# Merge of two branches formed in four spare PSUM banks, its rounded part made by ScalarE, and the next product started on every fourth merged block

## The chip, the cores and the metric

The kernel runs on one core of a Trainium2 chip. The metric is the device time of one execution, in microseconds (us). An engine here is TensorE (PE; its weight loads have a row of their own, PEld), VectorE (DVE), ScalarE (ACT), GpSimd (POOL) or SyncE (SP).

## What is computed

The reference runs two transformer-like blocks on 256 tokens of width 2048, all in fp32. The change is in the second block, at the place where two branches meet and go through an output product:

```python
merged = jax.nn.sigmoid(gate_ret) * (ret @ w_br_ret[l]) + jax.nn.sigmoid(gate_dil) * (dil @ w_br_dil[l])
x = x + merged @ w_out[l]
```

`ret` is 256 x 1024, `dil` is 256 x 512, `w_out` is 2048 x 2048. Ahead of it lie the first block, the projections, the retention and the dilated attention; behind it lie a cross attention to a memory of 256 tokens and a large expert layer, which is more than half of the time.

## The kernel before, in words

**Layout.** Activations are kept transposed: 128 partitions of the width by 256 tokens, `KC` = 16 such blocks for a width of 2048. A weight matrix is streamed as tiles of 1 MB (128 x 2048 numbers). SP loads them in one long order (`STREAM`) into a ring of four slots, and reloads a slot once both halves of its tile have been split.

**Split weights.** Products are made of a rounded part and a remainder. For each half of a tile (8 pieces of 128 x 128) ACT copies the half into `w_hi`, rounded (`split_half`, L1174; the copy is L1180), POOL forms `w_lo` = tile - `w_hi` (L427), and PE then runs the half. `w_hi` and `w_lo` have four places, so ACT may split a half once PE has done the half four before it (the wait on `half_done` in `split_half`). Activations are split in the same way into `h_hi` and `h_lo`. `half_wide` (L489) multiplies the rounded weight by both parts of the activation in one matmul of 512 columns (L495) and the remainder weight by the rounded part in one of 256 (L497). `half` (L478) does the same with three matmuls of 256 columns (L484, L485, L486).

**The stages around the change.** They follow each other in the weight stream: `gate`, `br_ret` (8 tiles), `br_dil` (4 tiles), `out2` (16 tiles), `kv`. PE holds results in PSUM banks 0 to 3, and DVE frees them by counting `bank_free`.
- In `gate`, 32 blocks are made into `pg`, and ACT puts a sigmoid on them.
- In `br_ret`, each half of a tile gives one block. DVE adds the two halves of its bank into a buffer `mrg` (L1718) and multiplies it by the gate in place in `pg` (L2449).
- In `br_dil` (PE from L1002), each half of a tile gives two blocks, of four pieces each. Half m (0 to 7) gives blocks 2m and 2m+1, in banks 2m mod 4 and 2m+1 mod 4. Before it writes block k, PE waits until DVE has read block k-4 out of the same bank.
- DVE (L2452 to L2468) takes each block k through four instructions, one after another, each behind a wait for the one ahead of it: the product of the bank and the gate into `mrg` (L2457), which frees the bank; the sum with the other branch, in `mrg` (L2459); the rounded copy into `h_hi` (L2461); the remainder into `h_lo` (L2463). The names `h_hi` and `h_lo` are parts of `hc_hl`, and so the trace calls them. Behind block 15 it raises `merged`.
- PE waits for `merged` (L1011), and then runs the 16 tiles of `out2` (`tile`, L530), each of which needs all 16 blocks of `h_hi` and `h_lo`. After each tile, DVE adds both halves of the bank to `x` (`added`, L2470; L2473 and L2475).
- ACT splits the weights of `br_dil` (L1517) and then those of `out2`, two tiles ahead of PE. Behind the third tile of `out2` it waits for `merged` and starts on the norm of the memory (L1520 on), whose arrays overlay `pg`.

Banks 4 to 7 of PSUM are not used from the end of the dilated attention until the norm of the memory, which uses bank 7 after the thirteenth tile of `out2`.

Of the kernel before, what the change touches and what calls it, by code (L numbers as in the profile page):

```python
# [19 lines left out]
F32 = mybir.dt.float32  # L20
# [4 lines left out]
ALU = mybir.AluOpType  # L25
ACT = mybir.ActivationFunctionType
# [3 lines left out]
T = 256  # L30
D = 2048
KC = D // P
# [52 lines left out]
FIRST = {}  # L85
# [3 lines left out]
RING = 4  # L89
# [30 lines left out]
def build(nc, a, out):  # L120
    ctx = ExitStack()

    def sem(name):
        return ctx.enter_context(nc.semaphore(name))

    psum = ctx.enter_context(nc.psum_tensor("psum", [P, 8, 512], F32))
# [23 lines left out]
    h_hl, c_hl = hc_hl[:, 0], hc_hl[:, 1]  # L150
    h_hi, h_lo, c_hi, c_lo = h_hl[:, 0], h_hl[:, 1], c_hl[:, 0], c_hl[:, 1]
# [93 lines left out]
    pg = at("pg", [P, GATE_TILES, T], 120)  # L245
    mrg = at("mrg", [P, 2, T], 200)
# [48 lines left out]
    bank_free, acc_free = sem("bank_free"), sem("acc_free")  # L295
# [36 lines left out]
    d_sc, d_mx, d_e, d_p, d_tp, d_pt, d_o, d_hi, d_lo = (sem("dil_" + n) for n in (  # L332
        "scores", "max", "exp", "prob", "turned", "prob_turned", "out", "hi", "lo"))
    s_sig = sem("gates_sigmoid")
    merged = sem("merged")
    k_half = sem("keys_done")
    m_tp, m_vn, m_sc, m_mx, m_e, m_p, m_pt_, m_pc, m_o, m_hi, m_lo = (sem("mem_" + n) for n in (
        "v_turned", "v_natural", "scores", "max", "exp", "prob", "turned", "prob_turned", "out", "hi", "lo"))
# [138 lines left out]
    def _(pe):  # L477
# [49 lines left out]
                                      start=s == 0, stop=s == 1)  # L527
            m.then_inc(norm_sum, 1)

        def tile(name, n, hl, after=None):  # L530

            pe.wait_ge(bank_free, bank_of[name] + n + 1)

            def moving(k):
                if after is not None and n == 0 and k % 4 == 0:
                    pe.wait_ge(norm_lo, 4 * NS[after] + k // 4 + 1)
                return hl[:, :, k]
            for h in range(2):
                half_wide(FIRST[name] + n, n % RING, h, lambda c: h == 0 and c == 0,
                          lambda c: h == 1 and c == KC // 2 - 1, lambda c: n % RING, lambda c: moving(h * 8 + c))  # L540
# [5 lines left out]
        for i in range(ADA_G):  # L546
            pe.wait_ge(ada_copied, i + 1)
            for j in range(RING):
                pe.wait_ge(landed[j], 16 * i + 16)
                wide = ring[:, j].rearrange("p k n -> p (k n)")  # L550
                for k in range(4):
                    m = pe.matmul(psum[0:2, 4 + i % 2, :], c_silu[:, 4 * j + k], wide[:, 512 * k:512 * k + 512],  # L552
                                  start=j + k == 0, stop=j + k == 6)
# [8 lines left out]
        for n in range(ADA_1):  # L562
            m = pe.transpose(psum[:, 6, 2 * n:2 * n + 2], mod_rows[:, n * P:n * P + P], const[0:2, IDENT, 0:2])
# [19 lines left out]
        for t in range(XBC):  # L583
            pe.wait_ge(bank_free, bank_of["xbc"] + t + 1)
            for h in range(2):
# [3 lines left out]
                for c in range(8):  # L589
                    k = h * 8 + c  # L590
# [4 lines left out]
                    m = pe.matmul(o, w_lo[:, slot, c], hc_hl[:, :, 0, k], start=False, stop=k == KC - 1)  # L595
# [47 lines left out]
        for g in range(2):  # L643
            for tb in range(2):
                m = pe.transpose(psum[:, 0, (2 * g + tb) * P:(2 * g + tb + 1) * P],
                                 xbc[:, 8 + g, 1, tb * P:tb * P + P], sq(IDENT))
# [8 lines left out]
        for c0, d, parts in sums:  # L655
            for n, (mat, tb) in enumerate(parts):
                m = pe.matmul(psum[:, 4, c0:c0 + 16], sq(mat), da[:, tb, d], start=n == 0, stop=n == len(parts) - 1)
# [4 lines left out]
        for n in range(4):  # L662
# [3 lines left out]
            for tb in range(2):  # L666
                pe.wait_ge(ssd_xw, 2 * n + tb + 1)
                m = pe.matmul(psum[:, (2, 6)[n % 2], :], b_nat[:, g, tb], xw[:, tb, :], start=tb == 0, stop=tb == 1)
# [67 lines left out]
        for g in range(2):  # L736
            for k in range(4):
                m = pe.matmul(psum[:, 6, g * T:g * T + T], sq(ONES), y_sq[:, 4 * g + k], start=k == 0, stop=k == 3)
# [232 lines left out]
        for m_ in range(2 * DIL_HG):  # L971
            h, tb = m_ // 2, m_ % 2
# [3 lines left out]
            for g in range(DIL_G):  # L976
                for s in range(tb + 1):
                    n = g * (tb + 1) + s
                    m = pe.transpose(flat[:, n * P:n * P + P], dil_s[:, m_ % 2, T * g + P * s:T * g + P * s + P],
                                     sq(IDENT))  # L980
# [5 lines left out]
            for n in range(last + 1):  # L986
                g, s = n // (tb + 1), n % (tb + 1)
                m = pe.matmul(psum[:, 2 + h % 2, tb * P:tb * P + P], v_dil[:, s, 4 * g + h], dil_pt[:, n],
                              start=n == 0, stop=n == last)
# [13 lines left out]
        for j in range(RING):  # L1003
            for h in range(2):
                def target(c):
                    if c % 4 == 0:
# [1 line left out]
                    return psum[:, 2 * h + c // 4, 0:T]  # L1008
                half(g0 + j, j, h, lambda c: c % 4 == 0, lambda c: c % 4 == 3, target,
                     lambda c: dil_hi[:, c % 4], lambda c: dil_lo[:, c % 4])  # L1010
        pe.wait_ge(merged, 1)  # L1011
        for n in range(KC):
            tile("out2", n, h_hl)
            if n == 12:
                norm_pe("mem", column=True)
        for n in range(KC):
# [6 lines left out]
        for n in range(8):  # L1023
# [3 lines left out]
            for k in range(4):  # L1027
                m = pe.transpose(psum[:, n % 2, k * P:k * P + P], kv[:, KC + 4 * g + k, mb * P:mb * P + P], sq(IDENT))
# [13 lines left out]
        for h in range(MEM_H):  # L1042
# [5 lines left out]
            for mb in range(2):  # L1048
                for tb in range(2):
                    m = pe.transpose(psum[:, h % 2, mb * T + tb * P:mb * T + tb * P + P],  # L1050
                                     mem_e[:, h % 2, tb, mb * P:mb * P + P], sq(IDENT))
# [4 lines left out]
            for c in range(4):  # L1056
                for mb in range(2):
                    m = pe.matmul(psum[:, 2 + c // 2, (c % 2) * T:(c % 2) * T + T], v_mem[:, mb, 4 * h + c],
                                  mem_pt[:, h % 2, mb], start=mb == 0, stop=mb == 1)
# [111 lines left out]
    def _(act):  # L1171
        st = Steps(act, act_step)
# [14 lines left out]
        def split_stage(name, first=0, n=None, ahead=0):  # L1187

            g0, n = FIRST[name] + first, n or dict(STREAM)[name]
            for s in range(ahead, RING if ahead else 0):  # L1190
                split_tile(g0 + s, g0 // RING, s)
            with act.Fori(1 if ahead else 0, n // RING) as i:
                for s in range(RING):
                    split_tile(i * RING + (g0 + s), i + g0 // RING, s)
# [59 lines left out]
        for q in range(4):  # L1254
            for k in range(4 * q, 4 * q + 4):
                m = act.activation(c_hi[:, k], ctx_raw[:, k], ACT.Identity, scale=scales[:, 1, k:k + 1],
                                   bias=mod[:, k, 1:2])
# [167 lines left out]
        def split_at(g):  # L1425
            split_tile(g, g // RING, g % RING)
# [28 lines left out]
        for n in range(2, RET_TILES + 2):  # L1455
# [11 lines left out]
            if n >= 14 and n % 2 == 0 and n <= 28:  # L1467
                h = (n - 14) // 2
# [14 lines left out]
        for m_ in range(2 * DIL_HG):  # L1483
            h, tb = m_ // 2, m_ % 2
            keys = P * (tb + 1)
            act.wait_ge(d_mx, m_ + 1)
            s, n = (t_[:, m_ % 2] for t_ in (dil_s, dil_n))
# [26 lines left out]
        split_tile(FIRST["br_ret"] + 2, FIRST["br_ret"] // RING, 2)  # L1514
        split_tile(FIRST["br_ret"] + 3, FIRST["br_ret"] // RING, 3)
        split_stage("br_ret", RING, KC // 2 - RING)
        split_stage("br_dil")  # L1517
        act.wait_ge(norm_in, 64)

        def gained_squared(name, src, hi, k):  # L1520
# [9 lines left out]
                m.then_inc(norm_sq, 1)  # L1530

        for n in range(KC):
            split_at(FIRST["out2"] + n)
            if n == 2:
                act.wait_ge(merged, 1)
            if 2 <= n < 10:
                gained_squared("mem", mem_raw, mem_hi, 2 * n - 4)
                gained_squared("mem", mem_raw, mem_hi, 2 * n - 3)
# [14 lines left out]
        for h in range(MEM_H):  # L1553
            act.wait_ge(m_mx, h + 1)
            for tb in range(2):
                m = act.activation(mem_e[:, h % 2, tb], psum[:, 4 + h % 2, tb * T:tb * T + T], ACT.Exp,
                                   bias=mem_n[:, h % 2, tb:tb + 1], scale=r_col[:, CROSS, tb:tb + 1],
                                   accum_out=mem_n[:, h % 2, 2 + tb:3 + tb])
# [109 lines left out]
    def _(dve):  # L1668
# [782 lines left out]
        st.settle()  # L2451
        g0 = FIRST["br_dil"]  # L2452
        dve.wait_ge(bank_free, 4 + bank_of["br_dil"])
        for k in range(KC):
            dve.wait_ge(half_done, 2 * g0 + k // 2 + 1)
            t_, m_ = mrg[:, 0], mrg[:, 1]
            dve.tensor_tensor(t_, psum[:, k % 4, 0:T], pg[:, KC + k], ALU.mult).then_inc(bank_free, 1)  # L2457
            dve.wait_ge(bank_free, 4 + bank_of["br_dil"] + k + 1)
            st.did(dve.tensor_tensor(m_, t_, pg[:, k], ALU.add))  # L2459
            st.settle()  # L2460
            st.did(dve.tensor_copy(h_hi[:, k], m_))  # L2461
            st.settle()
            m = dve.tensor_tensor(h_lo[:, k], m_, h_hi[:, k].bitcast(F32), ALU.subtract)  # L2463
            if k < KC - 1:
                st.did(m)
                st.settle()
        m.then_inc(merged, 1)
        dve.wait_ge(merged, 1)  # L2468

        def added(name, n):  # L2470

# [413 lines left out]
```

## Time and profile before

| | us |
|---|---|
| median of 3 runs | 4730.65 (4725.55 to 4736.2) |
| the profiled execution, its own time | 4737.4 |
| span of the profiled execution, first to last instruction | 4735.6 |
| `br_dil` and the merge: PE's first matmul of it to its first of `out2` | 2457.12 to 2503.77 |

Every position in the tables further down is in microseconds from the start of the span. A row of the timeline gives start, duration, engine, line, operation, the output and the inputs by name, and in brackets how long the engine had stood idle before it and which instruction released it. "PEclk" is the TensorE clock that was granted in a stretch, as a share of full speed.

### The profile page before, as it was taken

What the parts mean: (1) busy time and instruction counts of PE and PEld (TensorE: products, weight loads), DVE (VectorE), ACT (ScalarE), POOL (GpSimd) and SP (SyncE); (2) the same over time, 40 slices, a digit from 0 to 9 for tenths busy, and PEclk for the clock granted to TensorE, in tenths of its full rate; (3) what the DMA queues carried; (4) which work ended last, traced back from release to release, by engine and by line L of the source; (5) the groups of instructions that cost most, each with busy time, mean ns of one, the idle gap of its engine ahead of it and who ended that gap; (6) DMA issues with size and microseconds to landing.
All of it is one profiled execution on the core that took longest, in us unless ns stands there. A gap on an engine that the chain in (4) does not pass through costs nothing.

```text
span 4735.6 us, 65884 instructions
## 1 busy us (share of the span) xinstructions
PE 4394.2 (93%) x24574; PEld 3679.7 (78%) x24574; DVE 2613.2 (55%) x3813; ACT 1731.0 (37%) x1875; POOL 3294.6 (70%) x1312
## 2 busy tenths in 40 slices
PE   8898988789999989996998998999999899999997
PEld 1676755678888878884887786889888788888876
DVE  3325775355545664314244512398867856875784
ACT  1234422333333343431543432443333333333433
POOL 0347740678888877881876783797887787788776
PEclk9998979889999999997999999999999999999999
DMA  8346750445445544551544452444454454454443
GB/s 312 123 183 243 300 189 9 151 161 183 180 179 184 181 157 160 184 186 45 187 177 142 166 189 98 169 170 161 177 185 171 159 186 172 161 180 177 173 163 125
DMA packets 111109, 804.92 MB, mean 170 GB/s; under 512 B 12903, under 2 KB 13192, under 8 KB 14088
## 3 DMA queue, kind: packets, MB, share of 16 engines
q1 hardware_dynamic: 108720, 787.30, 45.8%
q10 hardware_dynamic: 2200, 14.90, 0.9%
q8 instruction: 142, 2.33, 0.2%
q14 instruction: 47, 0.39, 0.0%
HBM read 800.06 MB, written 2.10 MB: 169 GB/s over the span
## 4 chain that ended last, share of the span: by engine, by line
PE 41%; POOL 29%; issue 21%; DVE 8%; ACT 1%; DMA 1%; POOLq 0%; DVEq 0%; SPq 0%; ACTq 0%
POOL w_lo L427 28%; PE psum L495 18%; PE psum L497 9%; PE psum L610 3%; PE psum L552 2%; DVE out_hl L2679 2%; DVE out_hl L2677 1%; DVE hid L2675 1%; POOL ada_acc L455 1%; PE psum L1104 1%; PE psum L593 1%; PE psum L484 1%; PE psum L595 1%; PE psum L594 1%; PE psum L485 1%
## 5 line engine op out<-in xcount | busy, mean ns | idle before, releaser
L427 POOL TENSOR_TENSOR w_lo<-ring,w_hi 128x1024 fp32r<-128x1024 f32 x1216 | 2944.3, 2425 | 1286.4 <-ACT w_hi L1180 1285.5
L1180 ACT ACTIVATE w_hi<-ring 128x1024 fp32r<-128x1024 f32 x1240 | 1310.2, 1060 | 2146.8 <-PE psum L497 1887.6
L495 PE MATMUL psum<-hc_hl,w_hi 128*128 128x512 f32 x5184 | 1852.6, 401 | 86.4 <-DVE hc_hl L2138 24.5
L497 PE MATMUL psum<-hc_hl,w_lo 128*128 128x256 f32 x5184 | 1453.8, 280 | 0.0
L495 PEld LDWEIGHTS psum<-hc_hl,w_hi 128*128 128x128 f32 x5184 | 982.0, 189 | 325.3 <-issue 55.9
L497 PEld LDWEIGHTS psum<-hc_hl,w_lo 128*128 128x128 f32 x5184 | 985.8, 190 | 2.0 <-issue 1.9
L495 PE MATMUL psum<-out_hl,w_hi 128*128 128x512 f32 x2048 | 725.0, 398 | 30.3 <-DVE x L2689 27.4
L497 PE MATMUL psum<-out_hl,w_lo 128*128 128x256 f32 x2048 | 577.5, 282 | 0.0
L495 PEld LDWEIGHTS psum<-out_hl,w_hi 128*128 128x128 f32 x2048 | 387.6, 189 | 123.1 <-DVE x L2689 28.3
L497 PEld LDWEIGHTS psum<-out_hl,w_lo 128*128 128x128 f32 x2048 | 390.7, 191 | 0.0
L495 PE MATMUL psum<-hid_hl,w_hi 128*128 128x512 f32 x1024 | 367.0, 402 | 19.6 <-DVE hid_hl L2192 12.2
L455 POOL TENSOR_TENSOR ada_acc<-ada_acc,ada_row 128x2048 f32<-128x2048 f32 x56 | 256.1, 4574 | 70.3 <-ACT ada_row L1291 64.8
L497 PE MATMUL psum<-hid_hl,w_lo 128*128 128x256 f32 x1024 | 289.0, 282 | 0.0
L495 PEld LDWEIGHTS psum<-hid_hl,w_hi 128*128 128x128 f32 x1024 | 194.6, 190 | 70.8 <-DVE hid_hl L2192 14.5
L2687 DVE TENSOR_TENSOR x<-psum,x 128x256 f32<-128x256 f32 x256 | 108.0, 422 | 245.7 <-PE psum L497 245.1
L610 PE MATMUL psum<-x,ring 128*128 128x256 f32 x1024 | 233.9, 389 | 8.7 <-DMA ring<-mixed 5.7
L610 PEld LDWEIGHTS psum<-x,ring 128*128 128x128 f32 x1024 | 197.5, 195 | 46.0 <-DMA ring<-mixed 8.2
L2677 DVE CAST out_hl<-hid 128x256 fp32r<-128x256 f32 x128 | 221.9, 1733 | 4.4
L2199 DVE SCALAR_TENSOR_TENSOR x<-psum,mod,x 128x256 f32<-128x256 f32 x224 | 108.4, 484 | 201.7 <-PE psum L497 197.7
L497 PEld LDWEIGHTS psum<-hid_hl,w_lo 128*128 128x128 f32 x1024 | 195.5, 191 | 0.0
L495 PE MATMUL psum<-mem_hl,w_hi 128*128 128x512 f32 x512 | 181.0, 399 | 9.4 <-POOL w_lo L427 9.4
L1291 ACT ACTIVATE ada_row<-ring,c_silu 128x2048 f32<-128x2048 f32 x64 | 126.7, 1998 | 80.2 <-DMA ring<-mixed 53.7
(440 smaller groups left out, 5559.1 us busy)
## 6 DMA issues: line engine op xcount, KB each, us to landing
ring<-stream SPq DMA_DIRECT2D x652, 1024.0 KB, 4.8
ring<-mixed SPq DMA_DIRECT2D x96, 1024.0 KB, 6.3
x<-x ACTq DMA_DIRECT2D x2, 2048.0 KB, 11.2
ctx_raw<-ctx ACTq DMA_DIRECT2D x1, 2048.0 KB, 9.8
mem_raw<-mem ACTq DMA_DIRECT2D x1, 2048.0 KB, 7.8
out<-x SPq DMA_DIRECT2D x4, 512.0 KB, 2.6
filt_w<-filt_w ACTq DMA_DIRECT2D x1, 1024.0 KB, 11.0
dft<-dft ACTq DMA_DIRECT2D x1, 1024.0 KB, 12.9
```

What stands on the lines that cost most here:

```text
L427: pool.tensor_tensor(w_lo[:, slot], ring[:, s, k], w_hi[:, slot].bitcast(F32), ALU.subtract).then_inc(lo_ready, 1)
L455: pool.tensor_tensor(ada_acc[:, n % 2], ada_row[:, 0] if k == 1 else ada_acc[:, n % 2], ada_row[:, k % 2], ALU.add).then_inc(ada_done, 2 i ...
L495: pe.matmul(psum[:, b, :].rearrange("p (s t) -> p s t", s=2), w_hi[:, slot, c], x_hl, start=start(c), stop=False, skip_group_check=True)
L497: m = pe.matmul(psum[:, b, 0:T], w_lo[:, slot, c], x_hl[:, 0], start=False, stop=stop(c), skip_group_check=True)
L552: m = pe.matmul(psum[0:2, 4 + i % 2, :], c_silu[:, 4 * j + k], wide[:, 512 * k:512 * k + 512], start=j + k == 0, stop=j + k == 6)
L610: m = pe.matmul(psum[:, (3, 7)[i % 2], 0:T], ring[:, (3 * i) % RING, k], x[:, k], start=k == 0, stop=k == KC - 1)
L1180: act.activation(w_hi[:, 2 * (s % 2) + h], ring[:, s, k], ACT.Copy).then_inc(hi_ready, 1)
L1291: act.activation(ada_row[:, t % 2], w, ACT.Copy, scale=c_silu[:, t % KC, 0:1]).then_inc(ada_scaled, 1)
L2199: dve.scalar_tensor_tensor(x[:, d], psum[:, 4 + d % 4, s * T:s * T + T], mod[:, gate + d, 0:1], x[:, d], ALU.mult, ALU.add).then_inc(acc_f ...
L2677: st.did(dve.tensor_copy(out_hi[:, j], hid[:]))
L2679: dve.tensor_tensor(out_lo[:, j], hid[:], out_hi[:, j].bitcast(F32), ALU.subtract).then_inc(hid_ready, 1)
L2687: st.did(dve.tensor_tensor(x[:, d], psum[:, 4 + d % 4, 0:T], x[:, d], ALU.add))
```

## The change

The merged block is no longer formed in `mrg`. DVE writes the product of bank and gate into one of PSUM's banks 4 to 7 (block k in bank 4 + k mod 4) and adds the other branch there in place. ACT makes the rounded part `h_hi` out of that bank, and DVE makes `h_lo` from the bank and `h_hi`, three blocks later than the sum. A bank is written again once the `h_lo` of four blocks before is done. `merged` now counts blocks, and PE, in the first tile of `out2`, waits for 4, 8, 12 and 16 of them, at every fourth piece. ACT's splits of `br_dil` and of the first two tiles of `out2` are written out as 12 halves, and behind the halves 5 to 11 the rounded copies of two blocks each are put (blocks 2m-10 and 2m-9 behind half m), the last two blocks behind those.

```diff
-    merged = sem("merged")
+    merged, br_sum, br_hi = sem("merged"), sem("branches_summed"), sem("branches_hi")
...
-        def tile(name, n, hl, after=None):
+        def tile(name, n, hl, after=None, each=None):
 
             pe.wait_ge(bank_free, bank_of[name] + n + 1)
 
             def moving(k):
                 if after is not None and n == 0 and k % 4 == 0:
                     pe.wait_ge(norm_lo, 4 * NS[after] + k // 4 + 1)
+                if each is not None and n == 0 and k % 4 == 0:
+                    pe.wait_ge(each, k + 4)
                 return hl[:, :, k]
...
-        pe.wait_ge(merged, 1)
         for n in range(KC):
-            tile("out2", n, h_hl)
+            tile("out2", n, h_hl, each=merged)
...
-        split_stage("br_dil")
+
+        def merged_high(q):
+
+            for k in (2 * q, 2 * q + 1):
+                act.wait_ge(br_sum, k + 1)
+                act.activation(h_hi[:, k], psum[:, 4 + k % 4, 0:T], ACT.Copy).then_inc(br_hi, 1)
+
+        for n in range(RING + 2):
+            for h in range(2):
+                split_half(FIRST["br_dil"] + n, n % RING, h, h == 0)
+                if n >= 2 and 2 * n + h > 4:
+                    merged_high(2 * n + h - 5)
+        merged_high(7)
...
         for n in range(KC):
-            split_at(FIRST["out2"] + n)
+            if n >= 2:
+                split_at(FIRST["out2"] + n)
             if n == 2:
-                act.wait_ge(merged, 1)
+                act.wait_ge(merged, KC)
...
+        def merged_low(k):
+
+            dve.wait_ge(br_hi, k + 1)
+            dve.tensor_tensor(h_lo[:, k], psum[:, 4 + k % 4, 0:T], h_hi[:, k].bitcast(F32), ALU.subtract).then_inc(merged, 1)
+
         for k in range(KC):
             dve.wait_ge(half_done, 2 * g0 + k // 2 + 1)
-            t_, m_ = mrg[:, 0], mrg[:, 1]
-            dve.tensor_tensor(t_, psum[:, k % 4, 0:T], pg[:, KC + k], ALU.mult).then_inc(bank_free, 1)
+            if k >= 4:
+                dve.wait_ge(merged, k - 3)
+            both_branches = psum[:, 4 + k % 4, 0:T]
+            dve.tensor_tensor(both_branches, psum[:, k % 4, 0:T], pg[:, KC + k], ALU.mult).then_inc(bank_free, 1)
             dve.wait_ge(bank_free, 4 + bank_of["br_dil"] + k + 1)
-            st.did(dve.tensor_tensor(m_, t_, pg[:, k], ALU.add))
-            st.settle()
-            st.did(dve.tensor_copy(h_hi[:, k], m_))
-            st.settle()
-            m = dve.tensor_tensor(h_lo[:, k], m_, h_hi[:, k].bitcast(F32), ALU.subtract)
-            if k < KC - 1:
-                st.did(m)
-                st.settle()
-        m.then_inc(merged, 1)
-        dve.wait_ge(merged, 1)
+            dve.tensor_tensor(both_branches, both_branches, pg[:, k], ALU.add).then_inc(br_sum, 1)
+            if k >= 3:
+                merged_low(k - 3)
+        for k in range(KC - 3, KC):
+            merged_low(k)
+        dve.wait_ge(merged, KC)
```

## Rows read from the trace of the kernel before

**Rows 1.** The page, busy time of each engine over the whole span.

```profile
PE 4394.2 (93%) x24574; PEld 3679.7 (78%) x24574; DVE 2613.2 (55%) x3813; ACT 1731.0 (37%) x1875; POOL 3294.6 (70%) x1312
```

**Rows 2.** Windows by stage: length, busy time of each engine, PEclk, DMA share, GB/s.

```profile
2430.00:2457.00 27.00, 27.00 (x157) 23.61 (x156) 10.85 (x20) 10.20 (x10) 23.82 (x11) 1.00 0.54 190
2457.00:2503.90 46.90, 30.15 (x195) 28.43 (x193) 42.38 (x66) 9.52 (x9) 22.95 (x10) 0.82 0.36 130
...
2470.50:2476.30 5.80, 4.80 (x22) 4.80 (x23) 5.35 (x14) 1.06 (x1) 0.70 (x1) 0.50 0.05 23
...
2503.70:2507.00 3.30, 3.23 (x10) 2.74 (x11) 0.02 (x1) 0.00 (x0) 0.00 (x0) 0.50 0.18 77
```

**Rows 3.** Waits from 2457 to 2512: us in total, times, longest us.

```profile
PE psum L484 <- DVE mrg L2457: 9.3, 6, 2.1
...
PE psum L495 <- DVE hc_hl L2463: 7.3, 1, 7.3
```

**Rows 4.** The tile `mrg`: count, duration ns min/median/max, first and last start.

```profile
L2457 DVE TENSOR_TENSOR mrg<-psum,pg x16: 424/424/425, 2460.3 to 2502.0; 128x256 f32<-128x256 f32 x16
L2459 DVE TENSOR_TENSOR mrg<-mrg,pg x16: 424/425/2266, 2460.7 to 2502.5; 128x256 f32<-128x256 f32 x16
L2461 DVE CAST hc_hl<-mrg x16: 293/294/2368, 2461.3 to 2503.0; 128x256 fp32r<-128x256 f32 x16
L2463 DVE TENSOR_TENSOR hc_hl<-mrg,hc_hl x16: 424/426/2596, 2461.6 to 2503.3; 128x256 fp32r<-128x256 f32 x16
```

**Rows 5.** Timeline of DVE in `br_dil`.

```profile
2460.29 0.42 DVE L2457 TENSOR_TENSOR mrg<-psum,pg 128x256 f32<-128x256 f32 x1 [1.61 <-PE psum L486]
...
2461.59 2.51 DVE L2463 TENSOR_TENSOR hc_hl<-mrg,hc_hl 128x256 fp32r<-128x256 f32 x1
...
2464.60 2.27 DVE L2459 TENSOR_TENSOR mrg<-mrg,pg 128x256 f32<-128x256 f32 x1
...
2483.86 0.42 DVE L2457 TENSOR_TENSOR mrg<-psum,pg 128x256 f32<-128x256 f32 x1
...
2485.56 0.42 DVE L2457 TENSOR_TENSOR mrg<-psum,pg 128x256 f32<-128x256 f32 x1
...
2503.29 0.43 DVE L2463 TENSOR_TENSOR hc_hl<-mrg,hc_hl 128x256 fp32r<-128x256 f32 x1
```

**Rows 6.** Timeline of POOL in `br_dil`.

```profile
2461.39 2.44 POOL L427 TENSOR_TENSOR w_lo<-ring,w_hi 128x1024 fp32r<-128x1024 f32 x1 [0.44 <-ACT w_hi L1180]
2464.20 2.38 POOL L427 TENSOR_TENSOR w_lo<-ring,w_hi 128x1024 fp32r<-128x1024 f32 x1 [0.38 <-ACT w_hi L1180]
```

**Rows 7.** Timeline of PE: first matmuls of halves 0 and 1, of `out2` tiles 0 and 1.

```profile
2457.12 0.28 PE L484 MATMUL psum<-dil_hi,w_hi 128*128 128x256 f32 x1
...
2459.99 0.28 PE L484 MATMUL psum<-dil_hi,w_hi 128*128 128x256 f32 x1
...
2503.77 0.79 PE L495 MATMUL psum<-hc_hl,w_hi 128*128 128x512 f32 x1 [7.25 <-DVE hc_hl L2463]
...
2510.96 0.40 PE L495 MATMUL psum<-hc_hl,w_hi 128*128 128x512 f32 x1
```

**Rows 8.** Timeline of DVE behind two later tiles of `out2`.

```profile
2522.25 0.42 DVE L2473 TENSOR_TENSOR x<-psum,x 128x256 f32<-128x256 f32 x1 [4.67 <-PE psum L497]
...
2527.80 0.42 DVE L2473 TENSOR_TENSOR x<-psum,x 128x256 f32<-128x256 f32 x1 [4.66 <-PE psum L497]
2528.26 0.42 DVE L2475 TENSOR_TENSOR x<-psum,x 128x256 f32<-128x256 f32 x1
2528.60 3.04 DVE L2207 SCALAR_TENSOR_TENSOR mem_hl<-mem_raw,cols,mem_hl 128x256 fp32r<-128x256 f32 x2
```

**Rows 9.** Groups by shape: xcount, busy us, mean ns, idle before.

```profile
L1180 ACT ACTIVATE w_hi<-ring 128x1024 fp32r<-128x1024 f32 x1240 | 1310.2, 1060 | 2146.8 <-PE psum L497 1887.6 <-PE psum L486 151.4 <-PE psum L595 81.2
...
L1492 ACT ACTIVATE dil_hi<-psum 128x256 fp32r<-128x256 f32 x4 | 1.5, 383 | 41.5 <-PE psum L988 41.5
...
L2633 DVE TENSOR_TENSOR psum<-psum,gate_t 128x256 f32<-128x256 f32 x2 | 0.9, 432 | 0.1
```

## The prediction

> **What bounds the kernel now.** I began with the page: PE is busy for 93% of the span and POOL for 70% [rows 1]. An average over a long kernel says little of one stage, so I cut the stretch around the merge into windows [rows 2]. From 2430 to 2457 PE is busy for 27.00 of 27.00 us at a granted clock of 1.00: `br_ret` runs at PE's pace. From 2457 to 2503.9 PE is busy for only 30.15 of 46.90 us at a clock of 0.82, while DVE is busy for 42.38. So DVE sets the pace of `br_dil`. The waits say where [rows 3]: six times PE's first matmul of a half or of its second block waits for DVE's L2457, which frees a bank (9.3 us), and `out2` then waits 7.3 us for the last remainder, L2463.
>
> Why is DVE slow? Where nothing disturbs it, one block takes 1.70 us (2483.86 to 2485.56) [rows 5], so two blocks take 3.40 us, and PE makes two in 2.87 us (2457.12 to 2459.99) [rows 7]. DVE is the slower one even then. Sixteen blocks would take 27.2 us. They took 2460.29 to 2503.72 = 43.4 us [rows 5]. The other 16.2 us are in eight instructions that last some 2 us longer than their like: four times L2463, twice L2459, twice L2461. Rows 4 show it by the distance of maximum and median (2596 against 426 ns, 2266 against 425, 2368 against 294). Two of the eight stand in rows 5 (2461.59 and 2464.60), and they end at 2464.10 and 2466.87, just behind POOL's subtractions, which end at 2463.83 and 2466.58 [rows 6]. All eight go with a POOL subtraction in this way. L2457 is never among them: 424, 424, 425 ns for all 16 [rows 4]. It is the one of the four that reads PSUM and so has one input in SBUF. The others read only SBUF.
>
> PE pays twice more. After its waits the clock granted is 0.50, that is 1.2 in place of 2.4 GHz, from 2470.5 to 2476.3 and again in the first tile of `out2` [rows 2], which takes 7.19 us (2503.77 to 2510.96) [rows 7] where a tile takes 5.55 us (2522.25 to 2527.80) [rows 8].
>
> **The change, part by part.**
>
> *DVE.* Four instructions per block become three, and each of the three reads one input from PSUM. Product and sum write to PSUM from PSUM and SBUF. L2633 has exactly this form and size and takes 432 ns [rows 9]; L2457, the nearest form of the remainder's, takes 424 ns [rows 4]. An instruction that waits for the one ahead starts 0.46 us after it (2527.80 to 2528.26), one that doesn't 0.34 us (2528.26 to 2528.60) [rows 8]. The sum waits for the product, the remainder three blocks back waits for nothing fresh, and the next product waits for that remainder: 0.46 + 0.34 + 0.46 = 1.26 us a block, 2.52 us a half. If all three steps are full ones it is 1.38 and 2.76 us. Both lie below PE's 2.87 us, so DVE no longer holds a bank back. I take the eight long instructions as gone, because L2457 meets POOL in the same stretch and never shows one. If they stay, see the third case.
>
> Rows put reads from PSUM and from SBUF at the same 424 ns [rows 4]. The Trainium skill (VectorE: DVE Perf Modes, section on the TRN2 errata) states a fixed part of 120 cycles for a PSUM source and 58 for an SBUF source, which is 65 ns apart and speaks against moving two instructions of each block to PSUM. By that page, as an estimate, DVE would need up to 3.02 us a half, and the sum below would be some 1.5 us smaller. The measured 424 ns decides here.
>
> *ACT.* It takes on 16 rounded copies out of PSUM. The nearest row, `dil_hi` from PSUM, is 383 ns [rows 9]. With its split of 1.06 us [rows 9] ACT has 1.06 + 2 x 0.38 = 1.83 us to do in each 2.87 us, and in this stretch it was busy for only 9.52 of 46.90 us [rows 2]. The copies of half q stand behind the split of half q+5, which waits until PE has done half q+1. DVE asks for the first of them at block 2q+3, which is of half q+1 too, behind five other instructions, some 2.1 us after that half's end, and ACT needs 1.06 + 0.38 = 1.4 us. So DVE waits for nothing, or for tenths of a us. What is queued behind a copy is the next split, and behind that POOL and PE. POOL's remainder for half 4 is done at 2463.83 [rows 6] where PE, unhindered, needs it at 2457.12 + 4 x 2.87 = 2468.6. That is 4.8 us of reserve against at most 0.8 us of copies. Cost on the path: nothing; without that cover it would be 16 x 0.38 = 6.1 us.
>
> *PE.* Eight halves of 2.87 us end at 2480.08. The first tile of `out2` can start at once. It asks for remainders 0 to 7 (long done), 8 to 11 at 2480.08 + 2.77 = 2482.85 and 12 to 15 at 2480.08 + 4.16 = 2484.24. DVE starts on the last half's blocks 0.30 us behind PE, as it did at 2460.29 behind 2459.99, so at 2480.38. Remainder 11 is its third instruction there, done at 2481.6; remainder 15 is the ninth, done between 2484.0 and 2484.5. PE waits 0 to 0.3 us. The second tile then starts at 2480.08 + 5.55 = 2485.63, plus up to 0.3.
>
> *POOL, SP and the DMAs.* No subtraction or load is added. SP reloads a slot on POOL's remainder, and POOL must hold 2.87 us a half with 2.4 us of work [rows 6], as it did through `br_ret`. DMA was busy for a share of 0.54 at that full pace [rows 2], so loads do not bind when they come closer together.
>
> *Behind it.* The norm of the memory waits for tiles of `out2`, and everything after moves with them. I cost it at nothing.
>
> **The sum.** The second tile of `out2` starts at 2510.96 before [rows 7] and at 2485.6 to 2485.9 after, so 25.0 to 25.3 us are saved. It can be split into the 16.6 us of waits [rows 3], the 1.6 us that the first tile takes too long, and 7.1 us left for matmuls of `br_dil` at the clock of 0.50 and for gaps that no wait names. I take 25. Against the profiled execution's own 4737.4 us it gives 4712. That execution lies 6.8 us above the median of the three runs, 4730.65, and from the median it gives 4705.7, say 4706, which is my number.
>
> **The rivals.**
>
> *DVE stays the bound, mildly.* If a write to PSUM and its read back by the next instruction cost more than rows 8 show, say 0.55 us a step (0.09 above the full one; L2633, at 8 ns above L2457, speaks for the lower end), 48 steps take 26.4 us. The last remainder is done at 2486.7 and the second tile starts 1.4 us later, at 2488.1. The saving is 22.9 us: 4708, or some 4710 if PE's short waits bring the clock of 0.50 back for a few us.
>
> *The long instructions stay.* If POOL's subtractions hold one DVE instruction each, eight times 2.03 us come on top of 16 x 1.26 = 20.2 us: the last remainder at 2497.0, four pieces at half the clock (2 x 1.39 us), tile 1 at about 2499.8. The saving is 11.2 us: 4719. The 16 undisturbed L2457 speak against it.
>
> *The hand-over closes into a ring, and it is slower.* Place: ACT's queue, where copies wait for DVE's sums, DVE's next product for the remainder, the remainder for the copy, and the copy for a split that waits for PE. Should the three and five halves of distance not hold, one turn is PE 2.87 + DVE 2.76 + ACT 1.83 = 7.5 us a half. Eight of them and a tile are 65.5 us against 53.8 now (2457.12 to 2510.96), so 11.7 us slower: 4742. It decides from 6.0 us a half on. Against it: each wait reaches back at least three blocks.
>
> *The change does what it says and something behind takes it back.* DVE and POOL meet at other moments in the following stages, each meeting being worth 2 us (two instructions take 3.04 us at 2528.60 [rows 8]). A few more or fewer on a path that PE waits for are plus or minus 5 us, and I put this into the range. That nothing changes at all would need PE not to start `out2` early and DVE not to be faster. I see no way but a share of this case.
>
> **How the numbers follow.** Forecast 0.79, DVE mildly bound 0.09, long instructions stay 0.05, ring 0.02, taken back behind 0.05 (4715 to 4730). A measurement of this kernel tells about 0.2%, 9.5 us, from no change, so faster means under 4721. The first two cases lie there wholly, the third mostly: faster 0.93, the same 0.05, slower 0.02. The range: the three runs spread over 10.7 us, so a median may be off by some 4; with the 5 us behind, 4698 at the low end. At the high end 4719 takes in the dearer DVE and reaches the third case.
>
> **What would show it.** Right: three DVE instructions a block with none above 0.5 us in `br_dil`; block to block 1.26 to 1.38 us, with DVE waiting for PE at each half; copies near 0.38 us on ACT; PE from 2457 on busy throughout at a clock of 1.00, about 28.5 us from the first matmul of `br_dil` to the second tile of `out2`; no wait of PE on the merge above 0.5 us. Wrong: DVE instructions of 2 us again (third case), DVE rows waiting for ACT's copy by more than 1 us each half (ring), product and sum rows well above 432 ns (second), or a stretch behind `out2` that has grown.

## The result, and the profile after

The changed kernel takes 4708.25 us (median of 6 runs, 4702.76 to 4710.33) against 4733.42 us for the kernel before (6 runs, 4725.55 to 4737.32): 25.2 us less, a ratio of 0.9946 with a 95% interval of 0.9934 to 0.9958.

Below, "the passage" is the time from PE's first matmul of `br_dil` to its first of the second `out2` tile. It was 53.84 us before [rows 7]. Windows of the changed kernel (length, busy time of PE, PEld, DVE, ACT, POOL, then PEclk, DMA share, GB/s), the first of which is the passage:

```profile
2459.30:2488.20 28.90, 28.90 (x227) 28.16 (x226) 19.95 (x50) 15.09 (x26) 24.40 (x11) 1.00 0.52 183
2430.00:2457.00 27.00, 27.00 (x158) 23.80 (x157) 10.59 (x20) 9.89 (x11) 23.90 (x10) 1.00 0.54 194
2488.20:2511.00 22.80, 22.80 (x131) 19.76 (x131) 8.35 (x12) 14.31 (x25) 19.43 (x9) 1.00 0.53 188
2511.00:2533.00 22.00, 12.91 (x69) 10.96 (x68) 8.47 (x12) 7.75 (x14) 7.37 (x4) 0.84 0.22 86
```

PE was busy for 30.15 of 46.90 us at a clock of 0.82 [rows 2]. It is now busy for all 28.90 us at 1.00. DVE fell from 42.38 us of work to 19.95, ACT rose to 15.09, and neither sets the pace. The timeline of PE gives the corners of the passage (start, duration, engine, line, operation):

```profile
2459.33 0.28 PE L484 MATMUL psum<-dil_hi,w_hi 128*128 128x256 f32 x1
...
2482.36 0.40 PE L495 MATMUL psum<-hc_hl,w_hi 128*128 128x512 f32 x1
...
2488.01 0.40 PE L495 MATMUL psum<-hc_hl,w_hi 128*128 128x512 f32 x1
```

The eight halves take 23.03 us and the first tile of `out2` 5.65, so the passage is 28.68 us, 25.2 shorter. No wait of PE stands between them. Two blocks on DVE, from its timeline, to be laid beside [rows 5]:

```profile
2468.16 0.43 DVE L2478 TENSOR_TENSOR psum<-psum,pg 128x256 f32<-128x256 f32 x1 [0.86 <-PE psum L486]
2468.63 0.43 DVE L2480 TENSOR_TENSOR psum<-psum,pg 128x256 f32<-128x256 f32 x1
2468.97 0.41 DVE L2471 TENSOR_TENSOR hc_hl<-psum,hc_hl 128x256 fp32r<-128x256 f32 x1
2469.49 0.43 DVE L2478 TENSOR_TENSOR psum<-psum,pg 128x256 f32<-128x256 f32 x1
2469.95 0.43 DVE L2480 TENSOR_TENSOR psum<-psum,pg 128x256 f32<-128x256 f32 x1
2470.30 0.41 DVE L2471 TENSOR_TENSOR hc_hl<-psum,hc_hl 128x256 fp32r<-128x256 f32 x1
2471.04 0.43 DVE L2478 TENSOR_TENSOR psum<-psum,pg 128x256 f32<-128x256 f32 x1 [0.33 <-PE psum L486]
```

The brackets (the idle time in front of an instruction, and what ended it) have changed sides. Before, PE waited for DVE; now DVE waits for PE at each half, 1.61, 1.08 and 0.86 us at the first three (the first blocks have no remainder of an earlier block beside them), and 0.33 us from the fourth on. A block costs 1.33 us (2468.16 to 2469.49), and no instruction is long. The groups of the passage by shape (xcount, busy us, mean ns, idle before):

```profile
L2480 DVE TENSOR_TENSOR psum<-psum,pg 128x256 f32<-128x256 f32 x16 | 6.9, 432 | 0.6
L2478 DVE TENSOR_TENSOR psum<-psum,pg 128x256 f32<-128x256 f32 x16 | 6.9, 431 | 5.8 <-PE psum L486 5.2
...
L2471 DVE TENSOR_TENSOR hc_hl<-psum,hc_hl 128x256 fp32r<-128x256 f32 x16 | 6.4, 414 | 0.0
...
L1523 ACT ACTIVATE hc_hl<-psum 128x256 fp32r<-128x256 f32 x16 | 5.1, 373 | 0.4 <-DVE psum L2480 0.4
```

The profiled execution has a span of 4706.6 us, 29.0 less than before. Of that, 25.2 us lie in the passage. The passage starts 2.2 us later than before, and 6.0 us come from behind it. Those 6.0 us look like scatter and no part of the gain: in a second profile of the same kernel (span 4719.5 us) the stretch behind the passage is 8.1 us longer than before. The last section says where such differences come from.

### The profile page after: what moved, and what is told of

It is laid out like the page before. It is cut to its first block, busy times and chain, and to the rows that moved or that the text cites. A ratio compares the mean times of both kernels' runs of the same rounds, so it can differ in the third digit from the quotient of the medians.

```text
span 4706.6 us, 65879 instructions
## 1 busy us (share of the span) xinstructions
PE 4380.9 (93%) x24574; PEld 3673.3 (78%) x24574; DVE 2596.1 (55%) x3797; ACT 1735.5 (37%) x1891; POOL 3297.6 (70%) x1312
## 4 chain that ended last, share of the span: by engine, by line
PE 41%; POOL 29%; issue 21%; DVE 8%; DMA 1%; ACT 1%; POOLq 0%; DVEq 0%; SPq 0%; ACTq 0%
POOL w_lo L427 28%; PE psum L495 18%; PE psum L497 9%; PE psum L612 3%; PE psum L554 2%; DVE out_hl L2696 2%; DVE out_hl L2694 1%; DVE hid L2692 1%; PE psum L1105 1%; PE psum L595 1%; PE psum L596 1%; PE psum L597 1%; PE psum L484 1%; PE psum L485 1%; PE psum L486 1%
## 5 line engine op out<-in xcount | busy, mean ns | idle before, releaser
L495 PE MATMUL psum<-hc_hl,w_hi 128*128 128x512 f32 x5184 | 1853.7, 401 | 79.3 <-DVE hc_hl L2152 24.5
L495 PEld LDWEIGHTS psum<-hc_hl,w_hi 128*128 128x128 f32 x5184 | 980.8, 189 | 317.6 <-issue 55.7
L495 PE MATMUL psum<-out_hl,w_hi 128*128 128x512 f32 x2048 | 719.9, 395 | 31.8 <-DVE x L2706 28.4
L495 PEld LDWEIGHTS psum<-out_hl,w_hi 128*128 128x128 f32 x2048 | 387.3, 189 | 119.5 <-DVE x L2706 29.4
L495 PE MATMUL psum<-hid_hl,w_hi 128*128 128x512 f32 x1024 | 368.2, 403 | 18.9 <-DVE hid_hl L2206 12.2
L495 PEld LDWEIGHTS psum<-hid_hl,w_hi 128*128 128x128 f32 x1024 | 195.0, 190 | 70.6 <-DVE hid_hl L2206 14.4
L495 PE MATMUL psum<-mem_hl,w_hi 128*128 128x512 f32 x512 | 181.0, 399 | 9.4 <-POOL w_lo L427 9.4
## 6 DMA issues: line engine op xcount, KB each, us to landing
filt_w<-filt_w ACTq DMA_DIRECT2D x1, 1024.0 KB, 10.9
dft<-dft ACTq DMA_DIRECT2D x1, 1024.0 KB, 12.9
```

The lines of the kernel that those rows point to most:

```text
L495: pe.matmul(psum[:, b, :].rearrange("p (s t) -> p s t", s=2), w_hi[:, slot, c], x_hl, start=start(c), stop=False, skip_group_check=True)
```

## The experiments

The theory: DVE set the pace of `br_dil`, because of its four instructions a block and because POOL's subtractions held up those that read only SBUF; behind that, PE stood still at the hand-over. The rivals: that one part alone makes the gain (the early start, or ACT's copy), that the long instructions come from the chain of waits and not from POOL, and that the lag of three blocks is not needed. Every run was compared with the kernel before. The passage is read from one profile each, and it is the sharper measure: whole runs of one kernel spread over 10 us and more, while the two profiles of the changed kernel give 28.68 and 28.67 us.

| run | passage, us | beside before (53.84) | whole kernel, ratio (95% interval) |
|---|---|---|---|
| the change, again | 28.67 | -25.2 | 0.9947 (0.9932 to 0.9962) |
| late_start | 35.13 | -18.7 | 0.9952 (0.9935 to 0.9968) |
| dve_high | 32.43 | -21.4 | 0.9949 (0.9932 to 0.9967) |
| sbuf_sum | 40.14 | -13.7 | 0.9971 (0.9960 to 0.9982) |
| lag_zero | 38.00 | -15.8 | 0.9968 (0.9957 to 0.9980) |
| banks_only | 39.92 | -13.9 | 0.9961 (0.9946 to 0.9976) |
| early_only | 50.72 | -3.1 | 0.9990 (0.9978 to 1.0003) |
| sum_early | see below | | 0.9897 (0.9878 to 0.9915) |

**The change once more.** No edit.

> The changed kernel once more, as the measure for the runs beside it. Here and below, 'the passage' is the time from PE's first matmul of br_dil to its first of the second out2 tile: 53.84 us in the profile of before, 28.68 in the one of after. Main theory: the gain sits in this passage alone, so the passage is 28.5 to 28.9 again and the whole kernel 25 us, plus or minus 5, under before (ratio near 0.9947). Rival (the gain of the first measurement was partly luck behind the passage): passage the same, but the ratio away from 0.9947 by more than 0.001.

Passage 28.67 us and ratio 0.9947: as the theory had it.

**Sum and product in SBUF.** This tells the two theories of the long instructions apart, since order, waits and ACT's part stay and only the place of the sum moves.

```diff
+    mrg4 = at("mrg4", [P, 4, T], 184)
...
-                act.activation(h_hi[:, k], psum[:, 4 + k % 4, 0:T], ACT.Copy).then_inc(br_hi, 1)
+                act.activation(h_hi[:, k], mrg4[:, k % 4], ACT.Copy).then_inc(br_hi, 1)
...
-            dve.tensor_tensor(h_lo[:, k], psum[:, 4 + k % 4, 0:T], h_hi[:, k].bitcast(F32), ALU.subtract).then_inc(merged, 1)
+            dve.tensor_tensor(h_lo[:, k], mrg4[:, k % 4], h_hi[:, k].bitcast(F32), ALU.subtract).then_inc(merged, 1)
...
-            both_branches = psum[:, 4 + k % 4, 0:T]
+            both_branches = mrg4[:, k % 4]
```

> The change with product and sum in four buffers of SBUF in place of the four PSUM banks; ACT's copies, the lag of three blocks and the early start stay. Sum and remainder then read two inputs from SBUF. Main theory (POOL's subtraction, which also reads SBUF, holds up such an instruction until it ends): eight to ten of them last some 2 us longer, one for each POOL subtraction, so DVE needs 20.2 + 16 to 20 us, the passage is 41 to 46 us, 12 to 18 us slower than the changed kernel, and the products L2478 stay at 0.42 us. Rival (the long instructions came from the chain of waits in before and not from POOL): none of over 1 us, passage 28.7 us.

Eight long instructions came back, all of them the sum L2481 (from DVE's timeline; the products and remainders stay at 0.41 to 0.42 us):

```profile
2457.31 2.47 DVE L2481 TENSOR_TENSOR mrg<-mrg,pg 128x256 f32<-128x256 f32 x1
...
2460.15 2.46 DVE L2481 TENSOR_TENSOR mrg<-mrg,pg 128x256 f32<-128x256 f32 x1
...
2467.28 0.42 DVE L2479 TENSOR_TENSOR mrg<-psum,pg 128x256 f32<-128x256 f32 x1
2467.73 1.98 DVE L2481 TENSOR_TENSOR mrg<-mrg,pg 128x256 f32<-128x256 f32 x1
```

And POOL's timeline in the same run:

```profile
2457.10 2.40 POOL L428 TENSOR_TENSOR w_lo<-ring,w_hi 128x1024 fp32r<-128x1024 f32 x1 [0.44 <-ACT w_hi L1182]
2459.92 2.42 POOL L428 TENSOR_TENSOR w_lo<-ring,w_hi 128x1024 fp32r<-128x1024 f32 x1 [0.42 <-ACT w_hi L1182]
...
2466.99 2.44 POOL L428 TENSOR_TENSOR w_lo<-ring,w_hi 128x1024 fp32r<-128x1024 f32 x1 [1.75 <-ACT w_hi L1182]
```

Each of the eight long sums starts after a subtraction of POOL has started and ends 0.27 or 0.28 us behind that subtraction's end (2459.78 against 2459.50, 2462.61 against 2462.34, 2469.71 against 2469.43). It doesn't take a fixed time longer: the one that starts later in the subtraction is shorter (1.98 us). The product at 2467.28 reads PSUM and one input from SBUF; it lies wholly inside the third subtraction and takes 0.42 us. The rival falls. What each subtraction costs DVE is what is left of it. No run took POOL's subtractions away or moved them; that they are what holds the sums is read from these ends and from the place of the operands. Nor do two inputs in SBUF make the difference: two of the eight long instructions of the kernel before are the copy L2461, which has one input, `mrg` in SBUF, and took 2368 ns where its median is 294 [rows 4]. What the held-up instructions share is that none of their inputs is in PSUM.

The passage is 40.14 us, under the 41 to 46 expected, and 11.5 us longer than with the banks. The eight long sums add 13.9 us to DVE's work and not 16 to 20, because five of them lasted 1.98 us. The last remainder comes 10.9 us later than in the change, since DVE's waits for PE took up the rest. The other 0.6 us lie behind it: the granted clock from 2490.6 to 2493.0 was 0.58.

**The banks alone.** The kernel before, with one line changed.

```diff
-            t_, m_ = mrg[:, 0], mrg[:, 1]
+            t_ = m_ = psum[:, 4 + k % 4, 0:T]
```

> The kernel before with product and sum in PSUM banks 4 to 7; rounded copy and remainder stay on DVE, start of out2 stays late. Main theory: the eight long instructions vanish, a block costs 4 x 0.46 = 1.84 us (the copy, from PSUM, 0.42 in place of 0.29), the last remainder comes 32.6 us into the passage, the passage is 38.2 to 39.8 us, 14.0 to 15.6 us faster than before, ratio 0.9967 to 0.9970. Rival (long instructions come from the chain of waits): they stay, and the passage is no shorter than 53 us.

The groups by shape in its `br_dil` have no long instruction any more. The copy, which reads PSUM now, takes 424 ns where its median was 294 [rows 4], but never 2368:

```profile
L2459 DVE TENSOR_TENSOR psum<-psum,pg 128x256 f32<-128x256 f32 x16 | 6.9, 432 | 0.5
L2457 DVE TENSOR_TENSOR psum<-psum,pg 128x256 f32<-128x256 f32 x16 | 6.9, 432 | 2.1 <-PE psum L486 1.6
L2463 DVE TENSOR_TENSOR hc_hl<-psum,hc_hl 128x256 fp32r<-128x256 f32 x16 | 6.8, 424 | 0.5
L2461 DVE CAST hc_hl<-psum 128x256 fp32r<-128x256 f32 x16 | 6.8, 424 | 0.6
```

A block costs 1.85 us (products at 2448.14 and 2449.99), expected 1.84. The last remainder came 32.7 us into the passage (expected 32.6), and the passage is 39.92 us, 0.1 us above the range. Its waits show what the other two parts of the change have still to take away:

```profile
PE psum L495 <- DVE hc_hl L2463: 7.1, 1, 7.1
```

**The copy back on DVE.**

```diff
-                if n >= 2 and 2 * n + h > 4:
-                    merged_high(2 * n + h - 5)
-        merged_high(7)
...
-            dve.wait_ge(br_hi, k + 1)
+            dve.wait_ge(br_sum, k + 1)
+            dve.tensor_copy(h_hi[:, k], psum[:, 4 + k % 4, 0:T]).then_inc(br_hi, 1)
+            dve.wait_ge(br_hi, k + 1)
...
-            if k >= 3:
-                merged_low(k - 3)
-        for k in range(KC - 3, KC):
-            merged_low(k)
+            merged_low(k)
```

> The change with the rounded copy back on DVE, read from the PSUM bank, four instructions a block one after another; ACT only splits weights. Main theory: no long instructions, since none has two inputs in SBUF; a block costs 4 x 0.46 = 1.84 us, two blocks 3.68 against PE's 2.87, so DVE sets the pace: last remainder 3.2 + 16 x 1.84 = 32.6 us into the passage, passage 34.0 to 35.4 us, 5.3 to 6.7 us slower than the changed kernel. Rival (handing the copy to ACT is the larger part of the gain): over 12 us slower. Rival (PE sets the pace either way): under 1 us slower.

Passage 32.43 us, 3.8 longer than the change. I had 5.3 to 6.7, because I took every step of a block as a full one of 0.46 us. DVE's timeline shows 1.73 us a block: the next product waits for nothing fresh and starts 0.34 us after the remainder has started.

```profile
2454.39 0.43 DVE L2477 TENSOR_TENSOR psum<-psum,pg 128x256 f32<-128x256 f32 x1 [1.61 <-PE psum L486]
2454.86 0.43 DVE L2479 TENSOR_TENSOR psum<-psum,pg 128x256 f32<-128x256 f32 x1
2455.32 0.42 DVE L2468 CAST hc_hl<-psum 128x256 fp32r<-128x256 f32 x1
2455.78 0.42 DVE L2470 TENSOR_TENSOR hc_hl<-psum,hc_hl 128x256 fp32r<-128x256 f32 x1
2456.12 0.42 DVE L2477 TENSOR_TENSOR psum<-psum,pg 128x256 f32<-128x256 f32 x1
```

DVE is the bound (3.45 us for two blocks against PE's 2.87), but mildly, since PE's first `out2` tile absorbs part of the lag: PE waits once more there, 2.1 us. The run takes ACT's copy and the lag away together, so it prices the pair. The whole kernel's ratio cannot tell this run from the change.

**The late start, and the early start alone.** The first takes the early start out of the change; the second puts it alone into the kernel before.

```diff
+        pe.wait_ge(merged, KC)
         for n in range(KC):
-            tile("out2", n, h_hl, each=merged)
+            tile("out2", n, h_hl)
```

> The change without its early start: PE waits for all 16 merged blocks in front of out2. Main theory (the early start is worth only what DVE lags behind PE at the end): DVE's last remainder comes 26.8 us into the passage as before, PE stands still for 3.8 us, and the passage is 32.5 us if the clock stays at 1.00 and 34.0 if the first tile runs at the low clock as it did in before: 3.8 to 5.4 us slower than the changed kernel. Rival (the early start is the larger part of the gain): over 10 us slower. Rival (it hides nothing): no more than 1 us slower.

PE stood still as expected, 3.8 us. But the passage is 6.5 us longer, not at most 5.4. The windows of this run (its halves, the standstill, the first tile) show why:

```profile
2459.14:2482.17 23.03, 23.03 (x194) 22.98 (x192) 16.58 (x41) 11.76 (x20) 19.48 (x9) 1.00 0.53 186
2482.17:2485.95 3.78, 0.15 (x2) 0.00 (x0) 3.37 (x9) 2.26 (x5) 3.25 (x2) 0.87 0.57 238
2485.95:2494.27 8.32, 8.32 (x32) 7.16 (x33) 0.00 (x0) 1.06 (x1) 1.57 (x1) 0.65 0.35 126
```

The granted clock fell near the end of the standstill (1.00 from 2482.17 to 2484.9, 0.50 from 2485 to 2491), so most of its low stretch lay over the tile: a mean of 0.65, and 8.32 us for a tile of 5.55. In the kernel before it was 7.19 us after a longer standstill [rows 7], because the clock had fallen earlier: it was 0.50 already from 2500.4 to 2503.7, and the mean over the tile was 0.77. I had taken 7.19 as the worst.

Not every standstill brought the clock down. PE waited 2.1 us before its last four pieces in the run with the copy back on DVE, and 2.4 us in the run without the lag (below), and the granted clock was 1.00 throughout (2478.0 to 2483.65 and 2493.0 to 2498.4).

The second edit; `tile` has the argument `each` as in the change, and ACT waits for `KC` merged blocks:

```diff
-        pe.wait_ge(merged, 1)
         for n in range(KC):
-            tile("out2", n, h_hl)
+            tile("out2", n, h_hl, each=merged)
...
-            m = dve.tensor_tensor(h_lo[:, k], m_, h_hi[:, k].bitcast(F32), ALU.subtract)
-            if k < KC - 1:
-                st.did(m)
-                st.settle()
-        m.then_inc(merged, 1)
-        dve.wait_ge(merged, 1)
+            dve.tensor_tensor(h_lo[:, k], m_, h_hi[:, k].bitcast(F32), ALU.subtract).then_inc(merged, 1)
+            dve.wait_ge(merged, k + 1)
```

> The kernel before with nothing but the early start: merged counts blocks, PE waits for 4, 8, 12 and 16 in the first tile of out2; DVE's four instructions in SBUF stay. Main theory: DVE still needs 43.4 us, so the last remainder comes 46.6 us into the passage; only four pieces are left behind it (1.4 us, or 2.8 at half the clock) in place of a tile of 7.19. Passage 48.0 to 49.4 us, 4.4 to 5.8 us faster than before, ratio 0.9988 to 0.9991. Rival (the early start is the larger part): over 12 us faster.

Passage 50.72 us, 3.1 us shorter; I had 4.4 to 5.8. `out2` starts early, 38.3 us into the passage, and then waits again. PE's timeline at the last group of four:

```profile
2497.39 0.79 PE L495 MATMUL psum<-hc_hl,w_hi 128*128 128x512 f32 x1 [5.16 <-DVE hc_hl L2464]
...
2498.19 0.63 PE L495 MATMUL psum<-hc_hl,w_hi 128*128 128x512 f32 x1
...
2500.11 0.63 PE L495 MATMUL psum<-hc_hl,w_hi 128*128 128x512 f32 x1
```

Behind the last remainder 2.8 us are left, as expected, four pieces at the low clock. But the last remainder itself came 47.9 us into the passage instead of 46.6: nine of DVE's instructions were long in this profile and not eight. So the early start by itself is worth 3.1 us in this profile, which the ninth long instruction made some 1.3 us smaller, and 6.5 us on top of the other parts. Whole runs don't show it by itself: the interval of the ratio reaches over 1.

**The lag of three blocks taken away.**

```diff
-            if k >= 3:
-                merged_low(k - 3)
-        for k in range(KC - 3, KC):
-            merged_low(k)
+            merged_low(k)
```

> The change with the remainder directly behind its sum, and so behind ACT's copy, in place of three blocks later. Main theory: each half's first copy stands behind a split that waits for PE's next half, so PE's wait for a bank is split 1.06 + copy 0.4 + remainder 0.46 + product 0.46 + about 0.25 of signals = 2.6 us behind the half before, against 1.44 us; a half takes 4.1 us in place of 2.87, six of them 7.4 us more, and the tail some more: passage 36 to 40 us, 7 to 11 us slower than the changed kernel. Rival (the closed ring of the prediction, all four stations one behind another): 7.5 us a half, passage over 60 us. Rival (the lag is not needed): no slower.

Passage 38.0 us, 9.3 us longer than the change; a half takes PE 3.9 to 4.2 us from the third on. The remainder waits for ACT's copy in every block, mostly for 1.0 and 0.45 us in turn (3.2 us at the first); the longer one is the first block of a half, whose copy stands behind a split (DVE's timeline):

```profile
2474.19 0.43 DVE L2480 TENSOR_TENSOR psum<-psum,pg 128x256 f32<-128x256 f32 x1
2475.62 0.42 DVE L2471 TENSOR_TENSOR hc_hl<-psum,hc_hl 128x256 fp32r<-128x256 f32 x1 [1.00 <-ACT hc_hl L1523]
...
2476.42 0.43 DVE L2480 TENSOR_TENSOR psum<-psum,pg 128x256 f32<-128x256 f32 x1
2477.30 0.42 DVE L2471 TENSOR_TENSOR hc_hl<-psum,hc_hl 128x256 fp32r<-128x256 f32 x1 [0.45 <-ACT hc_hl L1523]
```

So part of the ring of my third rival exists, but even with no lag it does not close to 7.5 us a half. That PE's half and ACT's split go on beside it is my explanation. The run takes away only DVE's three blocks of distance; ACT's copies still stand behind the split of half q+5, and no run closed that distance. It stays faster than before, by a ratio of 0.9968.

**What comes next, and a version that beats both.** The fourth window of the result (2511 to 2533) has PE busy for 12.91 of 22.00 us, and the same hole was there before (12.91 us from 2534 to 2556). The waits of the changed kernel from 2511 to 2650:

```profile
ACT ntmp L1541 <- DVE norm_part L1688: 28.8, 2, 14.5
...
PE psum L495 <- POOL w_lo L427: 18.5, 2, 9.4
```

ACT waits for a half-sum of squares of the memory norm, and of the cross norm, which DVE makes behind tile 6 although the squares are there before tile 4 is done. ACT's next splits stand behind that wait, so POOL and then PE run dry. Two changed conditions move both half-sums:

```diff
-            if n in (6, 10):
-                norm_half_sum("mem", (n - 6) // 4)
+            if n in (4, 10):
+                norm_half_sum("mem", (n - 4) // 6)
...
-            if n in (6, 10):
-                norm_half_sum("cross", (n - 6) // 4)
+            if n in (4, 10):
+                norm_half_sum("cross", (n - 4) // 6)
```

> The changed kernel, and on DVE the first half-sum of the squares of the memory norm and of the cross norm placed behind tile 4 of out2 and of kv, in place of tile 6. In the profile of the changed kernel ACT waits 28.8 us for these two sums, POOL and PE run dry, and the tile behind each takes 17.2 and 17.1 us (DVE rows 2522.13 to 2539.38 and 2625.39 to 2642.45) against 5.65. The squares are ready at 2507.6, before tile 4 is done (2511.9). Main theory: both waits vanish, 11.5 us are saved at each, 23 us in all: the kernel 20 to 25 us under the changed one, ratio to the kernel before near 0.990. Rival (DVE, which has the lower halves to make in the same tiles with instructions of some 2 us, becomes late with a bank and PE waits there): under 12 us saved. Rival (the squares of the next two blocks come too late for it, DVE waits on ACT): no gain.

4690.48 us (5 runs), a ratio of 0.9897 to the kernel before: 45.3 us faster than it, and 23.7 us under the changed kernel's 4714.22 of the earlier series, as expected. In the profiles, the stretch from DVE's first row of `out2` to its first of `kv` fell from 103.2 us (2488.28 to 2591.48) to 92.1 us (2487.86 to 2580.00), near the 11.5 us expected for one hole. ACT's wait fell to 10.5 us and did not vanish, as I had expected it to; PE's for POOL almost did (waits from 2480 to 2640):

```profile
ACT ntmp L1541 <- DVE norm_part L1688: 10.5, 2, 6.3
...
PE psum L495 <- POOL w_lo L427: 1.5, 1, 1.5
```

## Why the prediction was right

- *What bounds the kernel.* DVE by its work and by POOL's subtractions, shown by the two runs that move only the place of product and sum: banks in place of SBUF take 13.9 us off the kernel before, and SBUF in place of banks puts 11.5 us on the change. With the banks alone a block still costs 1.85 us, 3.7 us a half against PE's 2.87.
- *DVE.* Predicted 1.26 to 1.38 us a block, measured 1.33; 432 and 414 ns an instruction, as the nearest rows had it. The Trainium skill (VectorE: DVE Perf Modes, section on the TRN2 errata) would have made the remainder dearer once it reads PSUM; it took 414 ns against 426 from SBUF [rows 4], so here the trace does not agree. Eight halves of 3.02 us in place of 2.87 would be 1.2 us, and not the some 1.5 that the prediction gave.
- *ACT.* 373 ns a copy against 383 assumed. DVE never waited for a copy in the passage. That the lag of three blocks is needed for this cover is shown by the run without it (9.3 us).
- *PE.* Last remainder at 26.8 us into the passage, predicted 26.9 to 27.4; PE waits 0, predicted 0 to 0.3. Eight halves take 23.03 us, predicted 22.96.
- *The sum.* 25.0 to 25.3 us predicted, 25.2 in the passage and in the medians. The term that was off most is the `out2` tile, 5.65 us and not 5.55 (below). That the passage fell in the range is what the working earned, though the passage before is that of one profile: with a ninth long instruction, as in the early start alone, it would have been some 1.3 us longer. That the medians agree as closely is luck: the 95% interval of the ratio is 11 us wide, and the medians of the second series differ by 22.4 us (4736.66 and 4714.22). The number itself, 4706, stood on a median of 4730.65 us for the kernel before, three runs; over six it was 4733.42, so 4708.25 is 2.2 us above the forecast.
- *The split of the gain.* In this order: banks 13.9 us, ACT's copy with its lag 4.8 (39.92 to 35.13), early start 6.5 (35.13 to 28.67). In another order the shares differ: the early start alone gives 3.1, and ACT's copy with its lag gives 3.8 if it comes last (32.43 to 28.68). The early start saves more than its standstill of 3.8 us, because it also keeps PE's clock up.
- *The rivals.* "The long instructions stay" was priced at 11.2 us saved; the run that keeps them saves 13.7. The working of that rival ended its last remainder at 2497.0 where 36.4 us from 2460.29 make 2496.7. "DVE stays the bound" did not occur: a step with a write to PSUM was 0.47 us and not 0.55. "The hand-over closes into a ring" did not occur; with the lag taken away a half took 3.9 to 4.2 us and not 7.5. For "something behind takes it back" the two profiles of the changed kernel give 6.0 us less and 8.1 us more behind the passage than before, about what the prediction had allowed for (5 us either way).

## What to carry to other kernels

When GpSimd works on SBUF all the time, look at the spread of VectorE's durations, not at the mean: in these runs equal instructions that read only SBUF had a median of 0.42 us and a maximum of 2.6, and the long ones ended just behind GpSimd's. Forming the value in a free PSUM bank cost 8 ns an instruction instead. Hand a step to another engine with a lag of some blocks, so that nobody waits for what was queued last. And a standstill of PE can cost more than its length (3.8 us of it were followed by a tile 2.8 us too long, while 2.1 and 2.4 us left the clock alone), so judge its removal by the next tile's time too. Then look for the next hole in the same windows.

## What was not expected

At the same granted clock of 1.00, PE runs this kind of product at two paces. Tiles of `out2` in the kernel before came 5.55 us apart [rows 8]; in the changed kernel they come 5.65 apart (DVE's timeline):

```profile
2499.52 0.42 DVE L2490 TENSOR_TENSOR x<-psum,x 128x256 f32<-128x256 f32 x1 [4.76 <-PE psum L497]
...
2505.17 0.42 DVE L2490 TENSOR_TENSOR x<-psum,x 128x256 f32<-128x256 f32 x1 [4.77 <-PE psum L497]
```

Either pace is nearly always held from one pause of PE to the next, and which one a stretch gets differs between two profiles of the same kernel. Count PE's matmuls of 512 columns (L495) in sixteens, which is one tile's worth: the first profile of the changed kernel has 236 such groups at the fast pace (5.51 to 5.57 us) and 161 at the slow one (5.62 to 5.68), the second 184 and 218. Some 55 groups at 0.1 us each are 5 to 6 us of the 12.9 by which their spans differ (4706.6 and 4719.5). That is a large part of the difference between these two. That the scatter of the other runs, which made them a poor judge of single parts here, has the same source is likely and not shown. What picks the pace was not tried and stays open.
